# Differential attention: where a finished head's outputs are scaled, in ScalarE's queue and in VectorE's

## The reference, cut to what matters

```python
scores = einsum(q, k) * scale - slopes * dist
probs = softmax(where(allowed, scores, -inf))
weights = probs[:, :, 0] - lam * probs[:, :, 1]
out = einsum("bhqk,bhke->bqhe", weights, v)
out = rms_norm(out, sub_g) * (1.0 - lambda_init)
return x + (out * silu(gate)) @ w_out
```

## Time and profile before

| what | us |
| --- | --- |
| median of 3 runs | 1954.5 |
| lowest, highest | 1953.13, 1955.06 |
| the profiled execution, its time | 1955.12 |
| the profiled execution, its span | 1953.2 |
| PE busy | 1897.7 (97% of the span) |
| DVE busy | 1231.7 (63%) |
| ACT busy | 924.1 (47%) |
| the last layer's slots, from about | 1690 to 1946 |

### The profile page before, as it was taken

One profiled execution on the slowest core, in us unless ns is written; L12 is line 12 of the kernel. 1 busy time (PEld: TensorE's weight loads), 2 busy tenths in 40 slices (PEclk: granted clock), 3 DMA queues, 4 the chain that ended last, 5 costly groups with the idle time before them and its releaser, 6 DMA issues.

```text
span 1953.2 us, 26626 instructions
## 1 busy us (share of the span) xinstructions
PE 1897.7 (97%) x9236; PEld 1528.4 (78%) x9236; DVE 1231.7 (63%) x1827; ACT 924.1 (47%) x1568; POOL 354.2 (18%) x230
## 2 busy tenths in 40 slices
PE   5999999999999999999999999999999999999997
PEld 3778788888888766788888887788888887777776
DVE  8954443443449787643343459988777876778763
ACT  4864432332335576532232334455546554466662
POOL 6942100000045000200000045022122225000002
PEclk9999999999999999999999999999999999999999
DMA  5214233323332211233333332222222222222222
GB/s 206 48 29 129 88 98 95 97 96 97 97 97 87 87 35 53 87 97 97 97 97 97 97 97 90 83 76 76 68 85 76 76 76 87 76 67 65 75 65 76
DMA packets 54521, 166.96 MB, mean 85 GB/s; under 512 B 13216, under 2 KB 13344, under 8 KB 53920
## 3 DMA queue, kind: packets, MB, share of 16 engines
q1 hardware_dynamic: 54432, 165.78, 27.7%
HBM read 161.30 MB, written 2.10 MB: 84 GB/s over the span
## 4 chain that ended last, share of the span: by engine, by line
PE 80%; DVE 12%; ACT 4%; issue 2%; DMA 1%; DVEq 0%; SPq 0%; ACTq 0%
PE bank L183 14%; PE bank L184 14%; PE bank L185 14%; PE bank L1588 4%; PE bank L1590 4%; PE bank L1589 4%; PE bank L2227 2%; PE bank L2229 2%; PE bank L2228 2%; PE bank L1604 1%; PE bank L1606 1%; PE bank L1605 1%; DVE w_lo L203 1%; PE bank L1651 1%; PE bank L2321 1%
## 5 line engine op out<-in xcount | busy, mean ns | idle before, releaser
L203 DVE TENSOR_TENSOR w_lo<-raw,w_hi 128x1024 fp32r<-128x1024 f32 x286 | 359.3, 1256 | 430.0 <-ACT w_hi L195 427.9
L195 ACT ACTIVATE w_hi<-raw 128x1024 fp32r<-128x1024 f32 x289 | 305.3, 1057 | 384.3 <-DMA raw<-in_w_dram 384.1
L183 PE MATMUL bank<-x1h,w_hi 128*128 128x512 f32 x680 | 266.9, 393 | 1.2 <-DVE x1l L218 1.2
L184 PE MATMUL bank<-x1l,w_hi 128*128 128x512 f32 x680 | 265.0, 390 | 0.0
L185 PE MATMUL bank<-x1h,w_lo 128*128 128x512 f32 x680 | 264.9, 390 | 0.0
L183 PE MATMUL bank<-x0h,w_hi 128*128 128x512 f32 x640 | 250.5, 391 | 0.0
L185 PE MATMUL bank<-x0h,w_lo 128*128 128x512 f32 x640 | 249.0, 389 | 0.0
L184 PE MATMUL bank<-x0l,w_hi 128*128 128x512 f32 x640 | 249.0, 389 | 0.0
L232 POOL TENSOR_TENSOR sq<-h 128x512 f32 (+1 forms) x46 | 60.5, 1315 | 762.3 <-DVEq L974 659.9
L1588 PE MATMUL bank<-x1h,w_hi 128*128 128x512 f32 x384 | 152.7, 398 | 0.6 <-DVE w_lo L203 0.3
L183 PEld LDWEIGHTS bank<-x1h,w_hi 128*128 128x128 f32 x680 | 127.9, 188 | 29.0 <-DVE x1l L218 1.6
(11 more groups left out here) (441 smaller groups left out, 3571.6 us busy)
## 6 DMA issues: line engine op xcount, KB each, us to landing
raw<-in_w_dram SPq DMA_DIRECT2D x289, 512.0 KB, 3.6
h<-in_xT_dram SPq DMA_DIRECT2D x1, 2048.0 KB, 13.0
Ur<-in_xu_dram SPq DMA_DIRECT2D x8, 256.0 KB, 2.8
out_dram<-h SPq DMA_DIRECT2D x8, 256.0 KB, 2.3
const<-in_const_dram SPq DMA_DIRECT2D x1, 1028.0 KB, 14.9
B_st<-in_B_dram SPq DMA_DIRECT2D x1, 1024.0 KB, 7.6
C_st<-in_C_dram SPq DMA_DIRECT2D x1, 1024.0 KB, 15.0
p_in<-in_pT_dram SPq DMA_DIRECT2D x1, 1024.0 KB, 4.8
```

Of the source, the lines that this page charges most:

```text
L183: e.matmul(b, w_hi[:, w, k], xh[:, k], start=(k == 0), stop=False)
L184: e.matmul(b, w_hi[:, w, k], xl[:, k], start=False, stop=False)
L195: e.activation(w_hi[:, z], raw[:, z], ACT.Copy).then_inc(hi_split, 1)
L203: e.tensor_tensor(w_lo[:, z], raw[:, z], w_hi[:, z].bitcast(F32), ALU.subtract).then_inc(w_split, 1)
```

## The change

In a finishing slot, ScalarE's four copies move from behind the exponentials to directly behind the root, with both of their waits. VectorE's reciprocal moves from behind the weights to between neg and the weights. Nothing is added or removed.

```diff
@@ diff_vector @@
                         diff_maxima.next(e, 4 * j + q).took("neg", e.tensor_scalar(...))
+                H = head_at(n, FINISH_AT)
+                if H is not None:
+                    e.wait_ge(head_roots.sem, head_roots.at("sd", H))
+                    head_scales.took("rc", e.reciprocal(head_rg[:, H % 2], head_sd[:, H % 2]))
                 part = chunk_at(n - 2)
                 if part:
...
-                H = head_at(n, FINISH_AT)
-                if H is not None:
-                    e.wait_ge(head_roots.sem, head_roots.at("sd", H))
-                    head_scales.took("rc", e.reciprocal(head_rg[:, H % 2], head_sd[:, H % 2]))
                 dve_split(e, U_KV2 + n + AHEAD, 0)
@@ diff_scalar @@
                     head_roots.took("sd", e.activation(head_sd[:, H % 2], head_ss[:, H % 2], ACT.Sqrt, bias=eps5[:, :], scale=1.0 / LANES))
+                    e.wait_ge(head_scales.sem, head_scales.at("rc", H))
+                    e.wait_ge(head_turned.sem, head_turned.at("t", H - 1))
+                    for q in range(4):
+                        last = e.activation(Otok[:, q * LANES:(q + 1) * LANES], bank[5 + H % 2][:, q * LANES:(q + 1) * LANES], ACT.Copy, scale=head_rg[:, H % 2, q:q + 1])
+                    head_scaled.took("k", last)
                 part = chunk_at(n - 1)
...
-                H = head_at(n, FINISH_AT)
-                if H is not None:
-                    e.wait_ge(head_scales.sem, head_scales.at("rc", H))
-                    e.wait_ge(head_turned.sem, head_turned.at("t", H - 1))
-                    for q in range(4):
-                        last = e.activation(...)
-                    head_scaled.took("k", last)
                 act_split(e, U_KV2 + n + AHEAD, 0)
```

More of the change, by code:

```diff
@@ L2496, in diff_scalar @@
                     act_norm(e, 8, eps5)
-                H = head_at(n, FINISH_AT)
-                if H is not None:
-                    e.wait_ge(head_scales.sem, head_scales.at("rc", H))
-                    e.wait_ge(head_turned.sem, head_turned.at("t", H - 1))
-                    for q in range(4):
-                        last = e.activation(Otok[:, q * LANES:(q + 1) * LANES], bank[5 + H % 2][:, q * LANES:(q + 1) * LANES], ACT.Copy, scale=head_rg[:, H % 2, q:q + 1])
-                    head_scaled.took("k", last)
                 act_split(e, U_KV2 + n + AHEAD, 0)
```

## The result

| | before | with the change |
| --- | --- | --- |
| median | 1955.13 (7 runs) | 1960.13 (7 runs) |
| lowest, highest | 1953.13, 1956.84 | 1957.8, 1964.83 |
| profiled execution, its time and span | 1955.12, 1953.2 | 1957.8, 1955.9 |

The ratio is 1.0029, with a 95% interval of 1.0019 to 1.0038: the change makes the kernel slower, by 3.7 to 7.4 us. The medians are 5.0 apart. All medians and ratios here leave out two executions that took far longer at a low granted clock: one of e1 (4825.87 us, clock 0.392 of full speed) and one of before (2724.96, 0.655), which was measured beside e5 to e8.

A forecast was written before the change was run, and what follows sets the result against it. PE, busy 97% of the span, was taken to bound the kernel, through its work and waits. Terms 4.07 + 1.04 = 5.1 us, added to the 1954.5 median, gave 1959.6 us, range 1956.3 to 1962.0.

The forecast's parts named there:

- The chain from root over split to w1: ScalarE's root to split, then VectorE's line 203 to w1, then PE's transposes, which waited 0.66 us behind slot 14.
- c: ScalarE's bare wait for rc between root and copies in a finishing slot, 0.61 to 1.69 us where listed.
- the load behind the copies: Exp's table load on ScalarE doesn't overlap the copies ahead of it: 0.13 us added to each finish.
- The delays at PE: Later split reaches PE's w1 waits: 1.47, 1.33, 0.97, 0.30 at heads 0, 1, 2, 4, total 4.07 us; head 3 nothing.
- Heads 5 and 6: Adjacent finishing slots; the chain to PE's wait at 1899.23 gets 0.30 + 0.74 = 1.04 us longer, net 1.04.
- the 1.38 us: PE's wait for copies at 1891.07 goes, but returns at the last gate unit's evacuation, then at 1899.23.
- The sum: PE's total loss over all finishes: 4.07 + 1.04 = 5.1 us.
- the most of 7.2: Upper bound in us: head 3 pays too, and VectorE waits 0.2 to 0.3 for the root at seven finishes.
- Rival 1: Not slower: PE doesn't wait on VectorE's line 203, the 1.38 us gain is kept, 1953.1 us; chance 0.06.
- Rival 2: Delays in slots 12, 15 and 19 partly covered: sum 2.8 to 3.9 us, about 1957.9; chance 0.2.
- Rival 3: A bare table load on ScalarE costs 1.28 us extra at six finishes: 7.7 more, 1967.3 us; chance 0.02.
- Rival 4: PE's lateness meets weight loads or a bank that isn't free: 6.5 to 8 us, about 1962; chance 0.07.

The follow-up runs named there:

- e1: Against the kernel before, only VectorE's reciprocal rc moves between neg and the weights, ScalarE's queue as before: 1953.99 us, ratio 0.9996.
- e5: The full change measured once more, unaltered, with a second profile: 1962.71 us, ratio 1.0033 against the kernel before.
- e8: Against the kernel before, rc moved between neg and the weights, and ScalarE's split of the weight unit put ahead of the four copies: 1953.59 us, ratio 0.9991.
- e2: Against the kernel before, only ScalarE's copies move behind the root, rc stays behind the weights: 1980.27 us, ratio 1.0129.
- e4: The change made for heads 0, 1 and 2 only, the others as in the kernel before: 1959.79 us, ratio 1.0023.
- e3: The full change plus a one-column Exp behind the root in seven finishing slots, putting the table load ahead of the wait for rc: 1953.45 us, ratio 0.9994.

## Why the prediction was right

**What bounds.** The chain from root over split to w1 was read rightly: three trials of it (e2, e4, e3) moved PE's waits by what ScalarE's stretch from root to split moved. VectorE's waits before line 203 grew by 1.48, 1.35 and 1.00 us in slots 11, 14 and 18, where 1.5, 1.3 and 1.0 were forecast.

**c and the load behind the copies.** c was expected at 1.69, 1.20, 0.84, 1.33, 0.61 and measured at 1.69, 1.20, 0.84, 1.32, 0.61. The load started 0.02 us behind the end of the copies, with no overlap.

**The delays at PE.** Relative to slot 10's scores, PE took up the transposes of w1 later by 1.45 us in slot 12 (1.47 expected), by another 1.30 in slot 15 (1.33), 0.94 in slot 19 (0.97), 0.26 in slot 27 (0.30); behind head 3 nothing, as expected. 3.95 against 4.07.

**Heads 5 and 6.** To the first wait on h (1899.23 before, 1902.63 after) it was 0.96 against 1.04: and the 1.38 us was handed back, at the two places named.

**The sum.** So up to there it is 4.9, against 5.1. The stretch as a whole grew by only 4.4, because of slot 34, where the trace of before had waited 0.45 us longer than nearly every later one.

**What was missed.** A small slip first: 1954.5 and the most of 7.2 make 1961.7, where the range goes to 1962.0. The forecast of 1959.6 and the medians of 1960.13 and 1962.71 lie near each other, but the sum lacks a term: the fall of the granted clock behind waits of about 2 us, some 1.6 us each time in e4 and e5. That the number came out so near is in part luck: the profile behind the 4.4 has no such fall, and the 0.45 of slot 34 goes the other way. I had put "more queues up behind the longer chain" at 0.07 with another mechanism in mind, and never asked what a longer wait does to PE's clock. How much of it is in the medians isn't shown. Of the 16 executions of the change, the seven up to 1960.4 us have a mean granted clock of 0.997 or 0.998, the nine from 1961.8 up 0.996 or less; so the spread of 7 us goes with the clock, but it is the clock of the whole program, with falls such as those near 125 and 810 us in it, and the first of these is in the profile of before too.

**The rivals.** Rival 1 (not slower, the gain at 1891 kept) failed at both steps. Rival 2 (part covered) failed: each slot paid in full. Rival 3, a load that costs more than its row, failed: the exponentials started 0.01 us behind the load's end in slot 14, with nothing to hide behind. Rival 4 (more queues up behind the chain, 6.5 to 8 us) came near the time of e5, but not as it was meant: in the stretch PE has no wait for weights, and its only new wait for a bank is the one for the evacuation of the last gate unit, which the forecast names. The drain that the Trainium skill's page "ScalarE: Activation LUTs", section "What ACT_TABLE_LOAD costs", adds to each switch isn't in any trace here; the load's 1283 ns is.

The reason why copies "right behind the root" don't help is in e3: in all these kernels the root's reciprocal stands behind the maxima in VectorE's queue, so there is a gap on ScalarE at that place. Before, the load stood in it. A version with rc ahead of the maxima, where the copies could really follow the root, was not run.

## What to carry to other kernels

A table load belongs to the instruction behind it, and it can run while that instruction's input is still being made; before moving something between the load and the wait it hides in, look at what the wait becomes. If an engine must stand for a short result anyway, put the load there, with a one-column instruction of the next function if need be. And of a chain that ends in a wait of PE, ask two things: what each microsecond in it costs, and whether the wait gets long enough for PE's clock to fall: it did behind waits of 2 us and more here, though not each time.

## What was not expected of the hardware

In the stretch the granted clock fell from 2.4 to 1.2 GHz (windows rows of 4 to 5 us at 0.50 to 0.68) behind waits of PE of 1.97 to 3.24 us. It stayed low for three to four microseconds, once for some six, and cost 1.5 to 1.6 us, the long one 2.6, and nothing where PE had to wait for others anyway. Behind the same wait of 1.97 us it fell in two of three profiles (e4 and e5, not in the first of the change). Behind waits of up to 1.93 us none in the stretch shows it. But near 125 us it fell in the profile of before behind waits of 0.68 and 0.97 us with a few short matmuls between them, and not in that of the change behind the same: the length of one wait doesn't decide it. Useless transposes in the waits took 8 us off e2's median. What decides between two executions of one program stays open.
